# MLA rotary scores: both parts of the rotary query stacked in 128 rows, two products per chunk in place of three

## The reference, cut to what matters

```
def mla_shared_kv(h, kv_in_norm, w_dkv_kr, kv_norm, w_ukv, cos_r, sin_r):
    ckr = rms_norm(h, kv_in_norm) @ w_dkv_kr
    c_kv = rms_norm(ckr[..., :KV_LORA_RANK], kv_norm)
    k_rope = apply_rope(ckr[..., KV_LORA_RANK:], cos_r, sin_r)      # 64 wide, shared by all 8 heads
    ...
    q = (cq @ w_uq).reshape(bsz, s_len, B_HEADS, QK_NOPE_DIM + QK_ROPE_DIM)   # 128 + 64
    q_rope = apply_rope(q[..., QK_NOPE_DIM:], cos_rh, sin_rh)
        logits = (jnp.einsum('bqhd,bkhd->bhqk', qn, k_nope)
                  + jnp.einsum('bqhd,bkd->bhqk', qr, k_rope)).astype(jnp.float32) * scale
        p = jax.nn.softmax(logits, axis=-1).astype(v.dtype)
        return jnp.einsum('bhqk,bkhd->bqhd', p, v)
```

## Time and profile before

| what | value |
|---|---|
| time, median of 3 runs | 1919.76 us (1919.53 to 1922.3) |
| the profiled execution: its time | 1921.17 us |
| its span (first to last instruction) | 1918.9 us |
| granted clock of TensorE, mean | 0.996 of full speed |
| PE busy | 1882.9 us, 98% of the span, 11693 products |
| PEld busy | 1696.1 us (88%) |
| DVE busy | 1269.5 us (66%) |
| ACT busy | 826.8 us (43%) |
| POOL busy | 48.6 us (3%) |
| DMA, mean busy share of the 16 engines | 32% |

### The profile page before, as it was taken

One profiled execution on the slowest core, in us unless ns is written; L12 is line 12 of the kernel. 1 busy time (PEld: TensorE's weight loads), 2 busy tenths in 40 slices (PEclk: granted clock), 3 DMA queues, 4 the chain that ended last, 5 costly groups with the idle time before them and its releaser, 6 DMA issues.

```text
span 1918.9 us, 28856 instructions
## 1 busy us (share of the span) xinstructions
PE 1882.9 (98%) x11693; PEld 1696.1 (88%) x11693; DVE 1269.5 (66%) x1742; ACT 826.8 (43%) x1203; POOL 48.6 (3%) x55
## 2 busy tenths in 40 slices
PE   8999999999999999999999999999999999999998
PEld 7899988988889899988997999889988898999887
DVE  6888752477656887872287878722878488877423
ACT  6444342355545544352254444522655464434422
POOL 0000000011100000000000000000000000000000
PEclk9999999999999999999999999999999999999999
DMA  5343333322213333333333333333221233333331
GB/s 167 87 110 102 98 110 101 91 62 75 78 55 100 88 88 93 105 111 97 98 78 88 88 100 103 107 103 92 61 61 56 67 88 88 95 103 107 110 91 45
DMA packets 347399, 175.10 MB, mean 91 GB/s; under 512 B 18479, under 2 KB 346269, under 8 KB 347293
## 3 DMA queue, kind: packets, MB, share of 16 engines
q1 hardware_dynamic: 346528, 172.51, 32.1%
q10 hardware_dynamic: 764, 1.11, 0.2%
HBM read 171.50 MB, written 2.10 MB: 90 GB/s over the span
## 4 chain that ended last, share of the span: by engine, by line
PE 88%; DVE 9%; ACT 1%; issue 1%; POOL 0%; DMA 0%; SPq 0%; DVEq 0%; ACTq 0%
PE acc L1763 22%; PE acc L1764 22%; PE acc L1765 22%; PE duo L1763 7%; PE duo L1765 7%; PE duo L1764 7%; DVE wl L1101 1%; DVE sqs L1212 1%; DVE y L1159 1%; DVE xT L1166 1%; PE duo L1791 1%; DVE xg L1136 1%; DVE hT L1402 1%; PE acc L2005 1%; ACT wh L632 0%
## 5 line engine op out<-in xcount | busy, mean ns | idle before, releaser
L1763 PE MATMUL acc<-xg,wh 128*128 128x256 f32 (+1 forms) x1624 | 538.7, 332 | 6.2 <-DVE wl L1101 2.7
L1764 PE MATMUL acc<-xg,wh 128*128 128x256 f32 (+1 forms) x1624 | 532.1, 328 | 0.0
L1765 PE MATMUL acc<-xg,wl 128*128 128x256 f32 (+1 forms) x1624 | 531.8, 327 | 0.0
L1763 PEld LDWEIGHTS acc<-xg,wh 128*128 128x128 f32 x1624 | 310.2, 191 | 36.2 <-DVE wl L1101 3.1
L1764 PEld LDWEIGHTS acc<-xg,wh 128*128 128x128 f32 x1624 | 310.3, 191 | 26.8 <-issue 1.4
L1765 PEld LDWEIGHTS acc<-xg,wl 128*128 128x128 f32 x1624 | 310.1, 191 | 26.6
L1101 DVE TENSOR_TENSOR wl<-raw,wh 128x1024 fp32r<-128x1024 f32 (+2 forms) x204 | 235.1, 1165 | 136.1 <-ACT wh L632 135.2
L1763 PE MATMUL acc<-hT,wh 128*128 128x512 f32 (+1 forms) x704 | 255.6, 363 | 3.5 <-DVE wl L1101 3.5
L1764 PE MATMUL acc<-hT,wh 128*128 128x512 f32 (+1 forms) x704 | 255.2, 363 | 0.0
L1765 PE MATMUL acc<-hT,wl 128*128 128x512 f32 (+1 forms) x704 | 255.2, 363 | 0.0
L632 ACT ACTIVATE wh<-raw 128x1024 fp32r<-128x1024 f32 (+2 forms) x204 | 200.5, 1009 | 126.6 <-PE acc L1765 80.7
(11 more groups left out here) (263 smaller groups left out, 3130.5 us busy)
## 6 DMA issues: line engine op xcount, KB each, us to landing
raw<-in_ffn_w_dram SPq DMA_DIRECT2D x240, 512.0 KB, 4.6
raw<-in_ffn_w_dram SPq DMA_DIRECT2D x32, 384.0 KB, 3.5
raw<-in_moba_w_qkv_dram SPq DMA_DIRECT2D x24, 512.0 KB, 4.0
raw<-in_moba_w_o_dram SPq DMA_DIRECT2D x8, 512.0 KB, 4.1
raw<-in_mla_w_o_dram SPq DMA_DIRECT2D x8, 512.0 KB, 4.1
xin<-in_x_dram SPq DMA_DIRECT2D x4, 512.0 KB, 5.6
raw<-in_mla_w_dq_dram SPq DMA_DIRECT2D x4, 512.0 KB, 3.9
raw<-in_mla_w_uq_dram SPq DMA_DIRECT2D x8, 256.0 KB, 3.0
```

What stands on the lines that cost most here:

```text
L1763: t.matmul(dst, w_h, m_h, start=start, stop=False)
L1764: t.matmul(dst, w_h, m_l, start=False, stop=False)
L1765: return t.matmul(dst, w_l, m_h, start=False, stop=stop)
```

## The change

The rotary part of a query is still split into an upper and a lower part, but both now lie in one operand of 128 rows, 64 rows each. For the even head of a pair, rows 0 to 63 hold its upper part and rows 64 to 127 its lower part; for the odd head it is the other way round. Against a key that has its upper part in both halves of the rows (`key_hi`), one product gives upper by upper plus lower by upper. A second product, against a key with its lower part in the rows of the query's upper part and zeros in the others (`key_lo[i]`), gives upper by lower. So two products do what three did.

For that, the rows of the rotary unit come head by head: x1 and x2 of the even head, then x1 and x2 of the odd head. The loads of the rotary weights are two per unit and part in place of four, with runs of 64 columns in place of 32. The sine table is one load in place of four. The exchange of halves is now inside each head, four copies of 32 rows in place of two of 64 rows. In MLA's turn heads the two copies of the even head of the pair stand where the exchange stood, and the two for the odd head stand after the upper part of the next `kh`. The upper part of `qrT` takes two ACT copies of 64 rows in place of one of 128, the lower part two DVE subtractions of 64 rows in place of one of 128, each with its result in the other 64 rows than its operands. Of the key, ACT makes one upper part in place of two, DVE a remainder and two products of it with `row_half`. The scores of a head wait for its own lower part. In MoBA the exchange and the products stay as they were.

```diff
@@ loads
-                return ((0, even), (RH, odd), (2 * RH, even + RH), (3 * RH, odd + RH))
+                return ((0, even), (ROPE, odd))
@@ ACT
+            def exchange_head(o):
+                for i, j in ((o + RH, o), (o, o + RH)):
+                    s.activation(rope_q[2][j:j + RH], rope_q[0][i:i + RH], COPY).then_inc(swapped, 1)
...
-            for i, j in ((0, 0), (1, 2), (2, 1), (3, 3)):
-                s.dma_start(sinT[i * RH:(i + 1) * RH], rope_r[1, j * RH:(j + 1) * RH]).then_inc(table_in, 16)
+            s.dma_start(sinT[:], rope_r[1]).then_inc(table_in, 16)
...
-                exchange(table_ready, 3)
+                act.wait_ge(table_ready, 3)
+                exchange_head(0)
+                exchange_head(ROPE)
...
-            for i in range(2):
-                s.activation(krT[:, i, 0], ck[:, KK], COPY, scale=row_half[:, i:i + 1]).then_inc(cq_hi, 1)
+            s.activation(key_hi, ck[:, KK], COPY).then_inc(cq_hi, 1)
...
-                part(qrT[:, 0])
+                for i in range(2):
+                    part(qrT[ROPE * i:ROPE * (i + 1), i], T[3][ROPE * i:ROPE * (i + 1)])
...
-                    exchanged((h + 1) // 2)
+                    exchanged((h + 1) // 2, 0)
...
                 if nxt:
                     direct("k", h + 1, kh[:, 0])
+                if turn:
+                    exchanged((h + 1) // 2, 1)
                 softmax_exp(n)
@@ DVE
+            v.tensor_tensor(key_rest, ck[:, KK], f32(key_hi), ALU.subtract).then_inc(cq_lo, 1)
+            dve.wait_ge(cq_lo, KK + 1)
             for i in range(2):
-                v.scalar_tensor_tensor(out=krT[:, i, 1], in0=ck[:, KK], scalar=row_half[:, i:i + 1],
-                                       in1=f32(krT[:, i, 0]), op0=ALU.mult, op1=ALU.subtract).then_inc(cq_lo, 1)
+                v.tensor_scalar(key_lo[i], f32(key_rest), row_half[:, i:i + 1], None, ALU.mult).then_inc(cq_lo, 1)
...
-                v.tensor_tensor(qrT[:, 1], T[3][:], f32(qrT[:, 0]), ALU.subtract).then_inc(part_lo, 1)
-                parts[0] += 1
+                for i in range(2):
+                    rows, beside = slice(ROPE * i, ROPE * (i + 1)), slice(ROPE * (1 - i), ROPE * (2 - i))
+                    dve.wait_ge(part_hi, parts[0] + 1)
+                    v.tensor_tensor(qrT[beside, i], T[3][rows], f32(qrT[rows, i]), ALU.subtract
+                                    ).then_inc(part_lo, 1)
+                    parts[0] += 1
@@ PE
-                        ins = product(dst, qrT[:, 0, c * P:(c + 1) * P], qrT[:, 1, c * P:(c + 1) * P],
-                                      krT[:, rope, 0, 0:w], krT[:, rope, 1, 0:w], False, True)
+                        q_rows = qrT[:, rope, c * P:(c + 1) * P]
+                        t.matmul(dst, q_rows, key_hi[:, 0:w], start=False, stop=False)
+                        ins = t.matmul(dst, q_rows, key_lo[rope][:, 0:w], start=False, stop=True)
...
-                pe.wait_ge(part_lo, 2 * HEADS + h // 2 + 1)
+                pe.wait_ge(part_lo, 2 * HEADS + h + 1)
```

More of the change, by code:

```diff
@@ L522, in shared_kv @@
                     for c, src in rope_columns(KVR, KVR):
-                        sp.dma_start(raw[:, u % SLOTS, 0:UT // 2, c:c + RH],
-                                     dkv[:, part * UT // 2:(part + 1) * UT // 2, src:src + RH]
+                        sp.dma_start(raw[:, u % SLOTS, 0:UT // 2, c:c + ROPE],
+                                     dkv[:, part * UT // 2:(part + 1) * UT // 2, src:src + ROPE]
                                      ).then_inc(raw_full[u % SLOTS], 16)
@@ L608, in _ @@
             rsqrt(RT0[N_PRE3])
-            rope_add(4 * HEADS + 2, ck[:, KK])
+            rope_add(4 * HEADS + 4, ck[:, KK])
             rsqrt(RT0[N_CKV])
             post_norm(N_F2)
-            pool.wait_ge(cq_lo, KK + 2)
+            pool.wait_ge(cq_lo, KK + 3)
             causal_mask(3)
-            rope_add(4 * HEADS + 4, T[3])
+            rope_add(4 * HEADS + 8, T[3])
             rsqrt(RT0[N_CQ])
             for gg in range(1, HEADS // 2):
-                rope_add(4 * HEADS + 2 * (gg + 2), T[3])
+                rope_add(4 * HEADS + 4 * (gg + 2), T[3])
             post_norm(N_MLA)
@@ L1032, in _, with exchanged @@
             split(u + 6)
-            def exchanged(gg):
-                exchange(evacuated, r + mla_rr["r", gg] + 1)
+            def exchanged(gg, i):
+                act.wait_ge(evacuated, r + mla_rr["r", gg] + 1)
+                exchange_head(ROPE * i)
             def rotated(gg):
                 act.wait_ge(roped, 2 * HEADS + 2 + gg)
-                part(qrT[:, 0])
+                for i in range(2):
+                    part(qrT[ROPE * i:ROPE * (i + 1), i], T[3][ROPE * i:ROPE * (i + 1)])
             def direct(a, h, dst):
@@ L1048, in _ @@
             v_split(HEADS)
-            exchanged(0)
+            exchanged(0, 0)
+            exchanged(0, 1)
             direct("q", 0, qh[:, 0])
```

18 lines of the change are left out of this document (9 added, 9 removed).

## The result

The changed kernel takes 1925.99 us (median of 19 runs, 1924.26 to 1927.24), the kernel before 1921.91 us (19 runs, 1919.53 to 1923.33). The ratio is 1.0022, with a 95% interval from 1.0016 to 1.0029. The forecast was 1922.9 us and its range ended at 1925.4, so the time lies outside it, and the change costs 4 to 5 us where +3.1 was forecast.

What follows compares the result with a forecast made beforehand. PE held 88% of the last chain, but DVE and ACT waits were expected to absorb most product savings. Terms +1.3 +1.2 +0 +0.24 +0.24 +0.77 -0.65 gave +3.1 on the median 1919.76: 1922.9 us, range 1918.0 to 1925.4.

Steps and rivals of the forecast that it cites:

- KV stage: Key's exchange: two more ACT copies, hidden by nothing, delay the weights and PE: +1.3 us (0 to +1.3).
- (a): Sign in the KV stage: the exchange lasts 2.6 us and PE's wait for ckv_diag ends 1.3 later.
- Rival 3: KV stage: a second PE gap keeps TensorE's clock down for one more stretch; +5.5 us, 1925.2; chance 0.18.
- Head 0: First MLA head: later exchange and an extra DVE lower part delay qscale and the mask: +1.2 us.
- check b: Sign in MLA's first head: PE waits about 1.5 us before the scores; qscale, not PE, frees the mask.
- Turn heads: MLA heads 1, 3, 5: shorter scores gain nothing behind ACT's qh, and the odd head's exchange is free: 0.
- Check (d): Sign in heads 1, 3, 5: PE waits about 0.4 us before the value product; ACT's qh still follows the exchange.
- Heads 2, 4 and 6: DVE's extra lower part delays PE's last transposes and uses up idle time before the mask: +0.24, +0.24, +0.77 us.
- check (e): Sign in MLA's later even heads: DVE has no idle time before their masks, and PE waits in the transposes.
- (f): Sign on DVE in MLA: the two half-row steps start at least 0.7 us apart.
- Rival 1: MLA: DVE's half-row steps overlap as usual, so the sum is only +1.6 us, 1921.3; chance 0.22.
- Rival 2: MLA: all 5.2 us of removed products reach the end, KV takes 1.3: -3.9 us, 1915.9; chance 0.10.

Runs made afterwards that it cites:

- the first experiment: Kernel before, with the exchanges of the rotary key and first pair of heads in quarters (four 32-row copies, not two of 64): 1924.41 us, ratio 1.0015.
- The filled gap: Changed kernel with six extra 512-column products on TensorE in the gap ahead of head 0's scores: 1925.52 us, ratio to before 1.0022.
- the exchange ahead of the key copy: Changed kernel with the second half of the next pair's exchange before the key copy in heads 1, 3, 5: 1924.67 us, ratio to before 1.0020.
- the third product: Changed kernel with a third rotary product per chunk put back in all eight heads: 1929.32 us, ratio to before 1.0039.
- the late half: Changed kernel with the rotated query of each pair's odd head made one head later: 1922.57 us, ratio to before 1.0008.
- the reordered KV kernel: Changed kernel with the rotary key's exchange moved behind the scaled input tiles and weight parts: 1918.88 us, ratio to before 0.9987.

## Why the prediction was wrong

The sum was +3.1 and is +4.9 in like executions; two of its steps failed (head 0 by 0.8 us, the turn heads by 1.2), and its base was off.

- **KV stage, +1.3**: right, +1.4. (a) holds, and the first experiment shows that the copies alone do it. Rival 3's second clock stretch did not come *there*: PE's wait kept its length, and `ckv_diag` to the first summed weights stays at 31.4 us. That rival's time, 1925.2, was near the measured one by luck.
- **Head 0, +1.2**: wrong by 0.8. The step that failed is "they are 0.65 shorter, so they end 0.65 later than before, at about 1395.4": it took the scores at full clock behind a gap that the prediction itself put at 1.5 us (check b). The gap came as said (1.54 us), `qscale` moved as said, but the clock fell, the scores took 4.7 us, and the mask was freed by PE. I had weighed the clock only where a fall was already in the rows, as rival 3, and not where the change makes a new gap. The filled gap (-0.8 to -1.0) and the quarters in the kernel before show this.
- **Turn heads, 0 each**: wrong by 0.4 each, +1.2 together. The failing step is "The odd head's exchange falls into the time in which ACT waits for the maxima, and costs nothing". ACT paid nothing, but POOL's sum is released by that exchange and moved with it from beside DVE's mask onto the step behind the maxima. A moved step counts with everything that it releases. Check (d) holds in its own terms (PE waits 0.36 us before the value product; ACT's `qh` follows the exchange) and did not see this.
- **Heads 2, 4 and 6, +0.24, +0.24 and +0.77**: +0.17, +0.16 and +0.69. The sizes are right and check (e) holds, but the reason given for the first 0.24, that PE's transposes end last, is not what the rows show: the mask starts straight behind DVE's own steps, 0.18 later than before, and taking the second half-row step away gives 0.7 us back. That the two reasons differ by so little is luck.
- **Head 7, -0.65**: -0.58. Scores take 3.3 us (c).
- **DVE's joints** (f): two half-row steps take 1.40 to 1.41 us, with no overlap. Rival 1 is out. This agrees with the rule that the prediction took from the Trainium skill (VectorE: DVE Perf Modes, section "Two Vector instructions with no wait between them"); no run here turned the rule alone off.
- **The loads, 0**: the stage that has them is 0.3 us shorter. The cause was not tested.
- **Rival 2**: out. Of 5.2 us of products, 2.9 reach the end.
- **The base**: two of the three runs of before that the median came from (1919.53 and 1919.76) are among the three fastest of 19, which have their median at 1921.91. By medians the miss of 3.1 us is 2.15 from the base and 1.0 from the change. With +3.1 on 1921.9 the forecast would have been 1925.0, 1.0 below the measured time. The three runs were 2.8 us apart (1919.53, 1919.76, 1922.3), which should have widened the range upwards.

## What to carry to other kernels

When a change inserts idle time ahead of TensorE's work, price that work at both clock levels, not only where the trace already shows a fall. When a step moves, follow what it releases on every engine, GpSimd above all, and see which VectorE step it then lies beside. A wait that is on the path is best asked "does it have to stand here?": behind work that somebody waited for, four copies cost no more than two, and the move helped the kernel before as well (4.5 us; 6.8 in the changed one). Look at what the moved step then meets: here POOL's sum made DVE's scaling 1.1 us longer.

## What the runs showed of the hardware

- TensorE's granted clock fell from 1.00 to 0.50 behind gaps of only 1.53 to 1.54 us, themselves behind 0.95 us of one-column products, in the quarters kernel, in both traces of the changed kernel and, by the same gap, in those with the exchange ahead of the key copy, the third product and the late half; behind 1.57 us in the reordered KV kernel it did not. The same stretch of code can thus cost 0.8 us more or less. What decides it stays open.
- In MoBA, at 404 to 408 us, the clock falls in some executions of one and the same kernel and not in others (0.68 and 1.00 in the two traces of the changed one), which costs 2.0 us and fits its two groups of run times.
- Four ScalarE copies of 32 rows take 2.59 us, two of 64 rows 1.28, two of 128 rows 1.14: from 32 to 128 rows the price is nearly all per copy.
- GpSimd's sum of 128x512 took 1.30 us alone, and 2.08 and 3.39 beside VectorE's scaling, which rose from 4.49 to 5.56; a VectorE step of 4 elements per row rose from 0.16 to 0.56.
